# State-space stage of a hybrid decoder step: the portions of filling work divided anew

## The reference, cut to what matters

```python
(gq, gk, gv, gr, ga, mq, mk, mv, mo, mi, mf, su, za, zb, zc) = split_in(hn @ P['w_in'][l])
...
y_c, re_new, im_new = s5_ssm(su, s_re, s_im, ...)      # 32 groups of 16 channels, 64 complex modes each
merged = sigmoid(za)*(y_a @ w_branch_a) + sigmoid(zb)*(y_b @ w_branch_b) + sigmoid(zc)*(y_c @ w_branch_c)
```

## Time and profile before

| what | value |
|---|---|
| median of 3 runs | 2168.93 us (2167.36 to 2169.13) |
| the profiled execution | 2167.99 us, its span 2166.2 us |
| mean granted TensorE clock | 0.995 |
| busy over the span | PE 98%, DVE 58%, ACT 35%, POOL 14% |
| first transposes of pass 0, 1, 2, 3 | 170.25, 208.44, 246.41, 284.37 us |
| first product behind the four passes | 324.47 us |

### The profile page before, as it was taken

One profiled execution on the slowest core, in us unless ns is written; L12 is line 12 of the kernel. 1 busy time (PEld: TensorE's weight loads), 2 busy tenths in 40 slices (PEclk: granted clock), 3 DMA queues, 4 the chain that ended last, 5 costly groups with the idle time before them and its releaser, 6 DMA issues. The chain is left out here.

```text
span 2166.2 us, 35594 instructions
## 1 busy us (share of the span) xinstructions
PE 2124.2 (98%) x15110; PEld 2078.9 (96%) x15110; DVE 1249.0 (58%) x1664; ACT 752.6 (35%) x1073; POOL 296.7 (14%) x464
## 2 busy tenths in 40 slices
PE   7999999999999999999999999999999999999997
PEld 6899999999999999999999997999999999999996
DVE  6514756344456364235643232679999999864447
ACT  6313334332422322333322133344444444421113
POOL 6688930000100000000000000000000000000001
PEclk9999999999999999999999999999999999999999
DMA  7322115122422222335322143222222222353222
GB/s 274 124 72 75 60 55 189 50 90 80 148 100 79 75 85 81 115 128 185 127 79 87 49 185 156 78 77 78 80 81 83 72 79 83 116 197 110 85 68 79
DMA packets 66420, 222.81 MB, mean 103 GB/s; under 512 B 7584, under 2 KB 13136, under 8 KB 62576
## 3 DMA queue, kind: packets, MB, share of 16 engines
q1 hardware_dynamic: 46432, 130.15, 18.4%
q0 software_dynamic: 14688, 62.06, 7.7%
q10 hardware_dynamic: 5184, 28.98, 3.4%
HBM read 168.38 MB, written 51.78 MB: 102 GB/s over the span
## 5 line engine op out<-in xcount | busy, mean ns | idle before, releaser
L305 PE MATMUL ps<-XH,WH 128*128 128x352 f32 (+1 forms) x1752 | 566.7, 325 | 5.6 <-ACT STAGE L365 3.1
L306 PE MATMUL ps<-XL,WH 128*128 128x352 f32 (+1 forms) x1560 | 492.0, 320 | 0.0
L308 PE MATMUL ps<-XH,WL 128*128 128x352 f32 (+1 forms) x1752 | 371.4, 320 | 0.0
L305 PEld LDWEIGHTS ps<-XH,WH 128*128 128x128 f32 x1752 | 330.3, 189 | 14.3 <-issue 10.2
L299 DVE TENSOR_TENSOR WL<-WRAW,WH 128x1024 fp32r<-128x1024 f32 x133 | 171.0, 1285 | 270.4 <-ACT WH L294 269.0
L306 PEld LDWEIGHTS ps<-XL,WH 128*128 128x128 f32 x1560 | 294.5, 189 | 0.1
L308 PEld LDWEIGHTS ps<-XH,WL 128*128 128x128 f32 x1752 | 292.6, 188 | 0.0
L294 ACT ACTIVATE WH<-WRAW 128x1024 fp32r<-128x1024 f32 x133 | 140.8, 1058 | 327.1 <-PE ps L308 305.1
L305 PE MATMUL ps<-HX,WH 128*128 128x352 f32 (+1 forms) x480 | 152.5, 319 | 0.0
L306 PE MATMUL ps<-HX,WH 128*128 128x352 f32 (+1 forms) x480 | 150.8, 320 | 0.0
L2767 PE MATMUL ps<-B,WQ 128*128 128x258 f32 x528 | 138.2, 283 | 0.6 <-DVE WQ L3179 0.6
(11 more groups left out here) (621 smaller groups left out, 4633.2 us busy)
## 6 DMA issues: line engine op xcount, KB each, us to landing
WRAW<-in_wslabs SPq DMA_DIRECT2D x133, 512.0 KB, 3.6
WRAW<-in_wup SPq DMA_DIRECT2D x88, 256.0 KB, 2.7
scratch_spill<-STAGE SPq DMA_DIRECT2D x40, 516.0 KB, 2.7
ZS<-scratch_spill POOLq DMA_DIRECT2D x24, 516.0 KB, 5.4
scratch_h<-HOUT ACTq DMA_DIRECT2D x22, 516.0 KB, 3.1
HRAW<-scratch_h POOLq DMA_DIRECT2D x22, 516.0 KB, 5.9
XIN<-in_xT SPq DMA_DIRECT2D x8, 516.0 KB, 4.6
XR<-in_xT ACTq DMA_DIRECT2D x2, 2064.0 KB, 8.7
```

What stands on the lines that cost most here:

```text
L305: pe.matmul(out[t], WH[:, slot, w, :], xh(k, t), start=(k == 0), stop=False)
L306: pe.matmul(out[t], WH[:, slot, w, :], xl(k, t), start=False, stop=False)
L308: last = pe.matmul(out[t], WL[:, slot, w, :], xh(k, t), start=False, stop=(k == nk - 1))
```

## The change

The numbers of steps at the points of the S5 stage are divided anew. Nothing else is edited.

```diff
-FILL = [("w", 4 * KT)]
+FILL = [("w", 4 * KT - 3)]
 FILL += [(f"s{q}{p}", k) for q in range(4) for p, k in
-        (("a", 1), ("b", 2), ("c", 5), ("d", 5), ("f", 2), ("g", 1))]
+        (("a", 1), ("b", 2), ("c", 4), ("d", 4), ("f", 3 + q // 3), ("g", 2 + 2 * (q // 3)))]
```

## The result

The changed kernel takes 2179.79 us (median of 6 runs, 2174.85 to 2183.27) against 2169.03 for the kernel before (6 runs, 2167.36 to 2171.92): a ratio of 1.0046 with the interval 1.0036 to 1.0056. It is slower by 10.8 us, where 3.1 were forecast, and outside the range (2169.2 to 2175.8). The profiled execution took 2183.27, at the upper end of its runs; its span is 2181.5.

The account below looks back on a forecast made before the run. In S5, the later of PE and POOL decides up to line 1125 of pass 3: POOL, 0.5 us earlier than now. With + 3.6 behind it, + 3.1 on the median 2168.93 gave 2172.0 us, own range 2169.4 to 2174.6, 8-in-10 range 2169.2 to 2175.8.

Parts of the forecast that it names:

- Number of steps: S5 stage: none added or removed; three steps, 4.25 us of PE work, move behind line 1125 of pass 3.
- eviction waits removed: PE at group starts in S5: 3.37 us removed up to line 1125 of pass 3, 0.75 behind it.
- place of the low part: DVE's queue: the low part of the group ending in `b` stands ahead of the chain, which starts 1.46 us later.
- Sum for passes 0 to 2: 5.6: PE's waits for `HST` at `y`: 1.9, 2.6 and 1.1 us, with each DVE instruction at its duration of before.
- 3.3, 2.4 and 1.0, in sum 6.7: The same three `HST` waits in us, with DVE and POOL holding each other up by 0.86 per meeting.
- the first reckoning: `HST` waits in passes 0 to 2 with DVE durations unchanged: 1.9, 2.6 and 1.1 us.
- The hand play: DVE's two-SBUF-input instructions played through against POOL's: `HST` waits sum to 6.7 us, POOL's tables end at 287.4.
- POOL is later than PE, so line 1125 starts at 287.4: Pass 3: POOL's tables end after PE arrives (284.9 or 286.0), so line 1125 starts 0.5 us earlier than before.
- the 286.0 of the forecast: PE's arrival at line 1125 of pass 3, in us, if the `HST` waits sum to 6.7.
- the forecast's + 3.6 behind line 1125: Rest of the stage: + 4.25 us for three more steps, - 0.75 eviction wait, + 0.1 `HST` wait.
- Rival 1 (the DVE chain decides): DVE meets more POOL instructions per pass; at one more, `HST` waits 9.2 us; about 2174.5 us, chance 0.20.
- The page's rule on the shared port: Two-SBUF-input DVE and SBUF-reading GpSimd instructions exclude each other; speaks against the change, sum 6.7 rather than 5.6 us.

Follow-up runs that it names:

- run 9: The changed kernel plus 18 unread products between `ss` and `y` in each of passes 0 to 2: 2174.56 us (1.0031).
- run 1: The changed kernel with DVE's low part of the group ending in `b` moved behind the sum that makes `HST`: 2177.67 us (1.0043).
- run 2: The changed kernel with a new filling point `e` between `ss` and `y`, two steps taken from `f` and `g`: 2176.93 us (1.0034).
- run 11: The kernel before with the shift alone: `w` 29 instead of 32, pass 3 `f` 3 and `g` 3: 2176.73 us (1.0039).
- run 6: The changed kernel with `XP` (POOL's last three table instructions of passes 1 to 3) made by DVE: 2178.61 us (1.0046).
- run 4: The kernel before with six memsets ahead of DVE's chain in passes 0 to 2, making `HST` late: 2189.93 us (1.0097).
- run 7: The changed kernel with filling point `e` between `ss` and `y` and `XP` made by DVE instead of POOL: 2165.84 us (0.9985).
- run 8: The changed kernel with point `e`, `XP` on DVE, and the low part of the `b` group behind `HST`: 2177.6 us (1.0035).

## Why the prediction was wrong, step by step

- *Number of steps, eviction waits removed, place of the low part:* right. The eviction waits went, in full (4.12 us), and neither came back at `b` to `c`.
- *"Sum for passes 0 to 2: 5.6", "3.3, 2.4 and 1.0, in sum 6.7":* this term was too small. 3.13, 3.31 and 2.44 were measured, 8.88. Against the durations of the first reckoning (1.9, 2.6 and 1.1) the low part took 0.5, 1.0 and 0.0 us longer, and the chain's four instructions of two SBUF inputs together 1.0, 0.1 and 1.3. All four were longer in all three passes than in pass 3, where POOL rests (the sum 2.04 to 2.16 instead of 1.22). The hand play had this right in pass 0, within 0.2, and not in the two others.
- *The price of a wait: the term that is missing.* A wait was priced at its length in every line of the sum, and the clock at nothing, without a reason. Behind three waits of 2.4 to 3.3 us the products of `y` ran at half clock, 5.90 us in all; run 9 takes the idle time away, and the slow products with it. This is the larger part of the error of 7.7 us.
- *"POOL is later than PE, so line 1125 starts at 287.4":* this step failed. PE came at 296.17: the 286.0 of the forecast, 2.2 more of waits, 5.9 of slow products, 1.85 from ahead of the stage, and 0.2 that is left. Without the slow products it would have come at 290.3 (an estimate, 296.17 - 5.90), still 0.5 behind POOL. POOL's tables ended at 289.74, 2.3 us later than forecast and outside 285.7 to 289.1. But 1.8 of this stood there before the stage began: its tables of pass 0 ended at 158.28 instead of 156.48, and from there to the end it took 131.5 us in place of 131.4. Where PE is on time POOL does bind (runs 1 and 2, 6.3 us). But then the 4.4 us of half clock behind that wait were missing too: the forecast's + 3.6 behind line 1125 was 8.0.
- *Rival 1 (the DVE chain decides)* is what happened. It was given 0.20 and 2174.5; waits of 9.2 us were its case and 8.9 came. Its price also had no clock in it: 4.2 and 5.9 give 10.1, which is about the measured 10.8.
- *The page's rule on the shared port* (the Trainium skill, "SBUF — State Buffer", section "Who interferes with whom"), weighed in the prediction, agrees in its direction: the low part took 1.68, 2.24 and 1.25 us in passes 0 to 2, beside POOL, and 1.23 in pass 3 with POOL at rest.

What stays open: how short a wait still leaves the clock alone. Every wait of 1.96 us or more between 20 and 345 us of these profiles had slow products behind it. Among the shorter ones length does not decide: eviction waits of 0.75 (the kernel before) and 1.27 us (run 11), a wait for POOL of 1.14 (run 2) and one of 1.60 at line 758, ahead of the stage (run 11), left the clock alone. But in run 1 the products behind a wait of 0.82 us were slow (a pair at 191.88 took 0.58), and so were those behind one of 1.33 us in pass 2 of run 6 (`y` took 5.08 instead of 3.43). Both stood right behind `ss`, 1.7 us of products of 8 columns; but so did one of 0.75 us in run 2, and the clock stayed up. No run was made to settle it.

## What to carry to other kernels

On a TensorE-bound kernel a wait of 2.4 to 3.3 us costs about 1.7 times its length here (14.8 us for 8.9), one of 4.3 to 5.2 us about 1.35 times (run 4: 14.4 and 5.0), so before moving filling work ask of every consumer what its cover is after the move, to the last microsecond, and price what is left uncovered with the clock. A group end moved to a new place moves its work on the other engines ahead of whatever stands there: look at what chain that queue carries. Where two long chains run beside TensorE, curing one (here `HST`) shows the other (POOL's tables), and only both together gave the gain that the change was worth: 4.1 us of eviction waits on paper, 3.4 us in run 7.

## What the runs showed of the hardware

- The stretch 45 to 60 us, before and after, where nothing was changed:

```profile
45.00:60.00 15.00, 13.69 (x67) 10.67 (x66) 9.81 (x10) 7.42 (x9) 13.38 (x23) 1.00 0.68 234
```

```profile
45.00:60.00 15.00, 12.44 (x56) 9.86 (x55) 8.07 (x9) 6.59 (x9) 13.08 (x27) 0.89 0.62 223
```

- The clock falls behind a wait here too. At line 758 PE waited 1.07 us for DVE's low part before and 2.56 in the changed kernel, at 48.76 us, and the product behind it took 0.80 us instead of 0.50. In the 13 profiles this wait varies from 0.53 to 2.56 us; in the two where it is over 2 (2.56, and 2.35 in run 8) the clock of the stretch is 0.89, in the eleven others 1.00.
- It can fall without a wait as well. At 1183 us of run 7 PE goes through 18 products of one column (1.9 us), and the filling products behind them take 0.48 us instead of 0.32 for some 3 us; PE doesn't wait, and the granted clock from 1185 to 1190 is 0.66. In the kernel before the same products at 1186 us are followed by ones of 0.32, at a clock of 1.00. The waits of PE behind 345 us come to about 15 us in both.
- From the first product behind the stage to the end the same program took 1840.1 us in run 9 (2169.4 - 329.28), 1841.7 in the kernel before and 1846.9 in run 7 (2166.6 - 319.67). This difference of 6.8 us is of the size of the spread among the executions of one kernel (1.5 to 8.7 us in the runs above), and more than the gain of run 7, which therefore can't be read from single executions.
- Adding work to an idle stretch made the kernel faster (run 9).
